# Differential attention scores: distance and mask added by VectorE in the pass that takes the row maximum, the first map scaled by ScalarE

## The chip, the cores and the metric

One core of a Trainium2 chip runs the whole program. The metric is device time in microseconds (us); lower is better. TensorE multiplies, VectorE and ScalarE do the elementwise work, GpSimd and SyncE here mostly issue transfers. PSUM has 8 banks of 128 x 512 float32, which only TensorE's results need; everything else lies in SBUF.

## What is computed

Two transformer blocks on x (512 tokens x 1024). The change is in the differential attention of the second block, 8 heads, each with two maps of 64 dimensions:

```python
dist = (tpos[:, None] - kpos[None, :]).astype(jnp.float32)
bias = -slopes[:, None, None] * dist               # slopes: 2 ** -(head + 1)
s = jnp.einsum("bhmqd,bhmkd->bhmqk", qblk, kt).astype(jnp.float32) * scale
s = s + bias[None, :, None]
s = jnp.where(dist >= 0, s, -jnp.inf)
p = jax.nn.softmax(s, axis=-1)
a = (p[:, :, 0] - lam * p[:, :, 1]).astype(vt.dtype)
return jnp.einsum("bhqk,bhkd->bhqd", a, vt)
```

Around it the second block has a convolution of 31 taps over 1024 channels, a cross-attention to a memory of 256 tokens, and projections.

## The kernel before

All work is laid out by hand: each engine has its own list of instructions, in order, and semaphores between them. A weight chunk (128 columns of a 1024-row matrix) is loaded into one of four raw buffers by SyncE, split by ScalarE into a hi part (`wh`, L1102) and by VectorE into a lo part (`wl`, L1760), and multiplied by TensorE in three matmuls for each of its 8 pieces (L463 to L465). Four chunks have split buffers, so the split of a chunk follows the use of the one four places ahead of it.

The differential stage runs over 8 heads j (0 to 7), and in each over 4 tiles tt of 128 queries; a unit is u = 4j + tt and has w = 128 (tt + 1) keys and two maps m. TensorE's list (L828 to L849) puts the pieces of five weight chunks between the attention steps of a head: the queries and keys of the next head, the gate of the previous one, and two for the convolution's input. Ahead of tiles 0 and 2 stand the scores of two tiles at once (`diff_scores`, L788): three float32 matmuls for each map (L800), then one for each map that adds slope times distance from two rows in float16 (L804), then one that adds the causal mask in the last 128 columns (L807), which closes the bank. In tiles 1 and 2 it sums squares of the next head's queries and keys (L529, waiting for `squared`), in tile 1 it multiplies the previous head by its values; it transposes each unit's probabilities (L677, waiting for `prob_ready`) a tile later. A bank 2 to 5 holds one map of one unit.

VectorE's list for a unit (L2203 to L2264): negated maximum of each map (L2214); in tile 3 the lo parts of the next head's keys and queries (L2125, L2131); in tile 0 the lo part of an older output (L1891); in tiles 0 to 2 four steps of the convolution (`conv`, L2173, 512 columns each); then it waits until both exponentials have emptied their banks, takes the reciprocals of both sums in one instruction (L2235), multiplies the second by minus lambda (L2236), scales the first map (L2238) and adds the second (L2239). After that come the lo part of the previous unit's transposed probabilities (L1942), weight chunks (L1760), in tile 2 the lo part of the values (L1887, waiting for ScalarE's hi part L1329) and the next head's normalised queries and keys (L2137). `then` makes VectorE wait for its own instruction.

ScalarE's list (L1518 to L1574): both exponentials with their sums (L1546), then the copy of the previous unit's transposed probabilities (L1324); after these in tiles 0 and 1 the copy of new queries or keys (L1250) and their squares (L1485), in tile 2 the roots (L1128, L1130, each with a table load) and the hi part of the values (L1329), in tile 3 ahead of the exponentials the hi parts of keys and queries (L1480, L1481); weight chunks (L1102) in all tiles.

Of the kernel before, what the change touches and what calls it, by code (L numbers as in the profile page):

```python
# [26 lines left out]
F32R = mybir.dt.float32r  # L27
F16 = mybir.dt.float16
BF16 = mybir.dt.bfloat16
# [5 lines left out]
P = 128  # L35
# [16 lines left out]
K_IDENT, K_ONES, K_FREQ, K_BLOCKS, K_SEL = 0, 128, 256, 257, 385  # L52
K_COLS = 385 + 4 * P

# [83 lines left out]
for _h in range(4):  # L138
# [6 lines left out]
    "const_in": "identity, ones and frequencies loaded", "rows_in": "packed vectors loaded",  # L145
    "tables_in": "masks, distances, slopes and blocks loaded",
    "mem_in": "memory loaded", "x_in": "x loaded", "bcast_in": "lambdas and sinks loaded on every partition", "late_in": "positions, gate bias and gain",
# [14 lines left out]
    "v_hi": "values: hi", "v_lo": "lo", "memk_hi": "memory's keys of a head: hi", "memk_lo": "lo",  # L162
    "negmax": "negated row maxima", "expd": "exponentials of sinks", "prob_ready": "units' probabilities",
    "pt_hi": "units' transposed probabilities: hi", "tanhed": "tanh of gates' arguments", "mixed": "gated outputs in mx",
# [49 lines left out]
def constants():  # L214
    k = np.zeros((P, K_COLS), np.float32)
    b = np.zeros((P, 3 * P), np.float32)
    h = np.zeros((P, S + 8 * P), np.float32)
    i = np.arange(P)
    k[:, K_IDENT:K_IDENT + P] = np.eye(P)
    k[:, K_BLOCKS:K_BLOCKS + P] = (i[:, None] // HD) == (i[None, :] // HD)  # L220
    k[:, K_ONES:K_ONES + P] = 1.0
    b[:, 0:P] = np.where(i[None, :] > i[:, None], 0.0, MASKED)
    b[:, P:2 * P] = np.where(i[None, :] <= i[:, None], 0.0, MASKED)
    b[:, 2 * P:3 * P] = np.eye(P)
    for n in range(8):
        for part in range(2):
            k[HD * (n % 2) + 32 * part + n, K_SEL + n // 2 * P:K_SEL + n // 2 * P + P] = 1.0
    j = np.arange(S)
    for half in (0, HD):
        h[half, 0:S], h[half + 1, 0:S] = j - (S - P), -1.0  # L230
        for n in range(8):
            cols = slice(S + n * P, S + n * P + P)
            h[half, cols], h[half + 1, cols] = 2.0 ** -(n + 1), i * 2.0 ** -(n + 1)
    k[:, K_FREQ] = (10000.0 ** (-(i % (HD // 2)).astype(np.float64) / (HD // 2))).astype(np.float32)
    return k, b.astype(mybir.dt.np(BF16)), h.astype(mybir.dt.np(F16))

# [87 lines left out]
def build(nc, t, out):  # L324
    ctx = ExitStack()
    with ctx:
# [15 lines left out]
        def sem(name):  # L342
# [30 lines left out]
        ident_b = sb("ident_b", [P, P], BF16)  # L373
        dist, slopes, blocks, xk = shared([("dist", [P, S], F16), ("slopes", [P, 8, P], F16), ("blocks", [P, P], F32)],
                                          [("xk", [P, 2, 2, MEM], F32R)])
        vt = sb("vt", [P, VT_COLS])
# [77 lines left out]
        def _(pe):  # L454
# [151 lines left out]
            def unit_scores(u_):  # L606

                if u_ >= FOX:
                    if u_ % 2 == 0:
                        banded_scores(u_)  # L610
                    return
                c, r = divmod(u_, 8)
                if r in (1, 2, 3, 5, 7):
                    return
                if r == 0:
                    pe.wait_ge(s.q_lo, c + 1)
                    banks.wait_empty(pe, ("ka", c))
                if u_ == 0:
                    pe.wait_ge(s.cum_done, 1)
                    pe.wait_ge(s.sel_in, 16)  # L620
                    pe.wait_ge(s.tables_in, 16 * 5)
                tiles = (0, 1) if r == 0 else (r // 2,)
                for side in range(2):
                    banks.open(pe, 2 + side, ("S", u_ + side))
                for n, tt in enumerate(tiles):
                    at, w = scores_at(u_ + 2 * n)
                    q_ = slice(tt * P, tt * P + P)
                    for q, k in ((0, 1), (1, 0), (0, 0)):
                        for side in range(2):
                            half = slice(HD * side, HD * side + HD)  # L630
                            pe.matmul(ps[2 + side][:, at:at + w], qd[c % 2][half, q, q_], kp[c % 2][half, k, 0:w],  # L631
                                      start=(n, q, k) == (0, 0, 1), stop=n > 0, **({"skip_group_check": True} if n else {}))
                    for side in range(2):
                        half = slice(HD * side, HD * side + HD)
                        pe.matmul(ps[2 + side][:, at:at + w], sel[half, c, :], negcum[half, 0:w], start=False, stop=True,
                                  **({"skip_group_check": True} if n else {}))
                for n, tt in enumerate(tiles):
                    at, w = scores_at(u_ + 2 * n)
                    for side in range(2):
                        ins = pe.matmul(ps[2 + side][:, at + w - P:at + w], ident_b[:], masks[:, 1, :], start=False, stop=True,  # L640
                                        skip_group_check=True)
                        if n == len(tiles) - 1:
                            banks.close(ins, ("S", u_ + side))
                        else:
                            banks.where["S", u_ + 2 + side] = banks.where["S", u_ + side]
# [142 lines left out]
            def diff_scores(j, first):  # L788
# [5 lines left out]
                for u_, w, q_ in units:  # L794
                    for m in range(2):
                        banks.open(pe, 2 + 2 * (u_ % 2) + m, ("D", u_, m))
                    for n, (q, k) in enumerate(((0, 1), (1, 0), (0, 0))):
                        for m in range(2):
                            half = slice(HD * m, HD * m + HD)
                            pe.matmul(outs[u_, m], qd[j % 2][half, q, q_], kd[half, j % 2, k, 0:w], start=n == 0, stop=False)  # L800
                for u_, w, q_ in units:
                    for m in range(2):
                        half = slice(HD * m, HD * m + HD)
                        pe.matmul(outs[u_, m], slopes[half, j, :], dist[half, S - w:S], start=False, stop=True)  # L804
                for u_, w, q_ in units:
                    for m in range(2):
                        ins = pe.matmul(outs[u_, m][:, w - P:w], ident_b[:], masks[:, 1, :], start=False, stop=True,  # L807
                                        skip_group_check=True)
                        banks.close(ins, ("D", u_, m))

# [188 lines left out]
        def _(pool):  # L999
# [10 lines left out]
            pool.dma_start(ident_b[:], t["consts_b"][:, 2 * P:3 * P]).then_inc(s.tables_in, 16)  # L1010
            pool.dma_start(dist[:], t["consts_h"][:, 0:S]).then_inc(s.tables_in, 16)
            pool.dma_start(slopes[:].rearrange("p a n -> p (a n)"), t["consts_h"][:, S:S + 8 * P]).then_inc(s.tables_in, 16)
            pool.dma_start(blocks[:], t["consts"][:, K_BLOCKS:K_BLOCKS + P]).then_inc(s.tables_in, 16)
# [71 lines left out]
        def _(act):  # L1085
# [432 lines left out]
            for j in range(8):  # L1518
                for tt in range(4):
# [16 lines left out]
                    for m in range(2):  # L1536
# [7 lines left out]
                        else:  # L1544
                            banks.wait_full(act, pt_key(UNITS - 1))
                        banks.empty(act.activation(prob[:, u_ % 2 if m == 0 else 2, 0:w], ps[banks.where[key][0]][:, 0:w],  # L1546
                                                   ACT.Exp, bias=stat[:, 0, col:col + 1],
                                                   accum_out=stat[:, 1, col:col + 1]), key)
                    if u_ > 0:
                        diff_pt_hi(u_ - 1)  # L1550
# [165 lines left out]
        def _(dve):  # L1716
# [484 lines left out]


            for j in range(8):  # L2203
                for tt in range(4):
# [6 lines left out]
                    for m in range(2):  # L2211
                        col = (2 * u_ + m) % 16
                        banks.wait_full(dve, ("D", u_, m))
                        dve.reduce_max(stat[:, 0, col:col + 1], bank(("D", u_, m))[:, 0:w], AX, negate=True)\  # L2214
                           .then_inc(s.negmax, 1)
                    if j and tt == (2 if j < 7 else 1):
# [9 lines left out]
                    if tt < 3:  # L2226
                        conv(4, j if tt else j - 1)
                    if (j, tt) == (7, 0):
                        diff_pt_lo(u_ - 1)

                    col = 2 * u_ % 16
                    r = stat[:, 2, col:col + 2]
                    for m in range(2):
                        banks.wait_empty(dve, ("D", u_, m))
                    then(dve.reciprocal(r, stat[:, 1, col:col + 2]))  # L2235
                    then(dve.tensor_tensor(r[:, 1:2], r[:, 1:2], nlam, ALU.mult))  # L2236
                    p0 = prob[:, u_ % 2, 0:w]
                    then(dve.tensor_scalar(p0, p0, r[:, 0:1], None, ALU.mult))  # L2238
                    dve.scalar_tensor_tensor(p0, prob[:, 2, 0:w], r[:, 1:2], p0, ALU.mult, ALU.add)\  # L2239
# [270 lines left out]
```

## Time and profile before

| | us |
|---|---|
| median of 3 runs | 1177.5 (1177.03 to 1178.06) |
| the profiled execution | 1176.51 |
| its span, first to last instruction | 1174.7 |
| TensorE busy in the span | 1141.0 |
| VectorE busy | 815.1 |
| ScalarE busy | 586.9 |

The granted clock of TensorE is 0.996 on average. The differential stage lies between 417 and 705 us of the span; its heads 2 to 6 each take some 36.7 us. In a profile's row the first number is the start, the second the time until the end of the last instruction that is merged into it; an idle time of the engine before the row stands in brackets with what ended it. Matmuls overlap, so what one costs is read from the start of the next.

### The profile page before, as it was taken

The numbers are of one execution on the slowest core, as the hardware profiler recorded it, in microseconds if no ns is written. First come the engines' busy times: TensorE is split into PE (matmuls) and PEld (weight loads), VectorE is DVE, ScalarE is ACT, GpSimd is POOL, SyncE is SP. The second block draws the span as 40 slices with busy tenths as digits, with TensorE's granted clock in tenths as the row PEclk, the third lists the DMA queues.
The fourth block names the chain that finished last, engine by engine and source line by source line (L and its number), as shares of the span: only waits on it lengthen the run. The fifth ranks groups of instructions, "written<-read, shape, count | busy, mean of one in ns | idle before, by whom it ended". The sixth has DMA issues, their size and how long they took to land.

```text
span 1174.7 us, 16788 instructions
## 1 busy us (share of the span) xinstructions
PE 1141.0 (97%) x6375; PEld 948.0 (81%) x6380; DVE 815.1 (69%) x1352; ACT 586.9 (50%) x1064; POOL 64.2 (5%) x73
## 2 busy tenths in 40 slices
PE   5899999999999999999999999999999999999998
PEld 5899777766899977777777778888888888788898
DVE  5788555668575237888898885898788686853351
ACT  5663455456564455766657655324554223651320
POOL 1029400101000000000000000000000000000000
PEclk9899999999999999999999999999999999999999
DMA  9967222321454322212222143232222323223221
GB/s 343 345 223 273 91 72 73 90 63 37 148 180 157 108 72 72 72 37 90 72 90 73 36 144 126 72 108 90 90 73 84 132 81 109 97 73 108 104 85 46
DMA packets 36208, 130.41 MB, mean 111 GB/s; under 512 B 4272, under 2 KB 6576, under 8 KB 35616
## 3 DMA queue, kind: packets, MB, share of 16 engines
q1 hardware_dynamic: 32560, 112.74, 29.0%
q0 software_dynamic: 3280, 16.29, 4.2%
q8 instruction: 51, 0.84, 0.3%
q10 hardware_dynamic: 288, 0.31, 0.1%
q14 instruction: 29, 0.24, 0.1%
HBM read 121.72 MB, written 6.29 MB: 109 GB/s over the span
## 4 chain that ended last, share of the span: by engine, by line
PE 87%; DVE 6%; ACT 3%; issue 2%; DMA 2%; SPq 0%; POOL 0%; DVEq 0%; ACTq 0%
PE bank L463 26%; PE bank L465 25%; PE bank L464 25%; PE bank L529 2%; PE bank L677 2%; DMA raw<-in_chunks 2%; DVE wl L1760 1%; PE bank L800 1%; PE bank L705 1%; PE bank L631 1%; ACT qf L1164 1%; DVE ca L2173 1%; DVE stat L1915 0%; PE bank L807 0%; DVE cumt L2441 0%
## 5 line engine op out<-in xcount | busy, mean ns | idle before, releaser
L463 PE MATMUL bank<-hl,wh 128*128 128x512 f32 x888 | 361.7, 407 | 0.9 <-DVE u L2187 0.9
L465 PE MATMUL bank<-hh,wh 128*128 128x512 f32 x888 | 347.1, 391 | 0.0
L464 PE MATMUL bank<-hh,wl 128*128 128x512 f32 x888 | 346.2, 390 | 0.0
L1102 ACT ACTIVATE wh<-raw 128x1024 fp32r<-128x1024 f32 x185 | 191.1, 1057 | 188.9 <-PE bank L465 178.1
L1760 DVE TENSOR_TENSOR wl<-raw,wh 128x1024 fp32r<-128x1024 f32 x185 | 225.2, 1242 | 84.5 <-ACT wh L1102 84.1
L463 PEld LDWEIGHTS bank<-hl,wh 128*128 128x128 f32 x888 | 167.2, 188 | 37.9 <-issue 4.8
L465 PEld LDWEIGHTS bank<-hh,wh 128*128 128x128 f32 x888 | 166.6, 188 | 36.4
L464 PEld LDWEIGHTS bank<-hh,wl 128*128 128x128 f32 x888 | 167.3, 188 | 33.6 <-issue 3.1
L2173 DVE SCALAR_TENSOR_TENSOR ca<-u,vt,ca 128x512 f32<-128x512 f32 x232 | 157.9, 745 | 0.0
L464 PE MATMUL bank<-oh,wl 128*128 128x512 f32 (+1 forms) x256 | 93.9, 367 | 0.0
L465 PE MATMUL bank<-oh,wh 128*128 128x512 f32 (+1 forms) x256 | 93.9, 367 | 0.0
L463 PE MATMUL bank<-wl,hh 128*128 128x256 f32 x320 | 91.6, 286 | 0.7 <-DVE hl L2089 0.7
L464 PE MATMUL bank<-wh,hl 128*128 128x256 f32 x320 | 90.5, 283 | 0.0
L465 PE MATMUL bank<-wh,hh 128*128 128x256 f32 x320 | 90.5, 283 | 0.0
L463 PE MATMUL bank<-ol,wh 128*128 128x512 f32 x192 | 75.5, 393 | 0.0
L463 PEld LDWEIGHTS bank<-wl,hh 128*128 128x128 f32 x320 | 61.4, 192 | 1.8 <-issue 1.8
L464 PEld LDWEIGHTS bank<-wh,hl 128*128 128x128 f32 x320 | 61.4, 192 | 0.5 <-issue 0.5
L465 PEld LDWEIGHTS bank<-wh,hh 128*128 128x128 f32 x320 | 61.4, 192 | 0.0
L1546 ACT ACTIVATE prob<-bank,stat 128x128 f32<-128x128 f32 (+3 forms) x64 | 33.1, 523 | 49.2 <-DVE stat L2214 48.5
L463 PE MATMUL bank<-wl,oh 128*128 128x256 f32 x192 | 55.7, 290 | 1.0 <-DVE ytok L2050 0.7
L464 PEld LDWEIGHTS bank<-oh,wl 128*128 128x128 f32 x256 | 49.7, 194 | 8.0 <-issue 0.5
L465 PEld LDWEIGHTS bank<-oh,wh 128*128 128x128 f32 x256 | 49.5, 193 | 7.5
(323 smaller groups left out, 1676.2 us busy)
## 6 DMA issues: line engine op xcount, KB each, us to landing
raw<-in_chunks SPq DMA_DIRECT2D x193, 512.0 KB, 3.7
ada_a<-in_chunks SPq DMA_DIRECT2D x8, 512.0 KB, 10.9
ada_b<-in_chunks SPq DMA_DIRECT2D x8, 512.0 KB, 8.6
x<-in_x POOLq DMA_DIRECT2D x4, 512.0 KB, 10.5
mem_scratch<-kvm POOLq DMA_DIRECT2D x1, 2048.0 KB, 8.2
x<-in_x POOLq DMA_DIRECT2D x1, 2048.0 KB, 8.1
x_scratch<-x POOLq DMA_DIRECT2D x1, 2048.0 KB, 7.7
kvm<-mem_scratch POOLq DMA_DIRECT2D x1, 2048.0 KB, 9.5
```

What stands on the lines that cost most here:

```text
L463: pe.matmul(o, a[0], b[1], start=start, stop=False, **kw)
L464: pe.matmul(o, a[1], b[0], start=False, stop=False, **kw)
L465: return pe.matmul(o, a[0], b[0], start=False, stop=stop, **kw)
L529: ins = pe.matmul(ps[bank][:, 0:n], ones_[:], x_, start=i == 0, stop=i == len(squares) - 1)
L631: pe.matmul(ps[2 + side][:, at:at + w], qd[c % 2][half, q, q_], kp[c % 2][half, k, 0:w], start=(n, q, k) == (0, 0, 1), stop=n > 0, **({"sk ...
L677: ins = pe.transpose(ps[b][:, n * P:n * P + P], blk, ident[:])
L705: ins = pe.matmul(ps[7][half, cols], v_, p_, start=kb == 0, stop=True, skip_group_check=True)
L800: pe.matmul(outs[u_, m], qd[j % 2][half, q, q_], kd[half, j % 2, k, 0:w], start=n == 0, stop=False)
L1102: act.activation(wh[:, SLOT[nxt]], raw[:, RAW_SLOT[nxt]], ACT.Copy).then_inc(s.w_hi, 1)
L1546: banks.empty(act.activation(prob[:, u_ % 2 if m == 0 else 2, 0:w], ps[banks.where[key][0]][:, 0:w], ACT.Exp, bias=stat[:, 0, col:col + 1] ...
L1760: dve.tensor_tensor(wl[:, w], raw[:, RAW_SLOT[nxt]], wh[:, w].bitcast(F32), ALU.subtract)\
L2173: ins = dve.scalar_tensor_tensor(dst, src, w, dst, ALU.mult, ALU.add)
```

## The change

The distances are no longer two float16 rows with a table of slopes, but one float32 table of 128 x 512: minus half the distance for head 0, and -1e30 where a key is behind its query. VectorE adds it to the scores: one instruction (`tensor_tensor_reduce`) writes minus the sum back to PSUM and takes the minimum of it, which is the negated maximum. The exponential takes the scores with scale -1. After tile 3's pass of each head but the last, VectorE halves the table. TensorE's matmuls with slopes and mask go, and each score bank closes with the last of its own three matmuls. On VectorE the four convolution steps of tiles 0 to 2 become 1, 1 and 2, with the first reciprocal between the first two and the second behind the second; ScalarE, behind both exponentials, waits for the first reciprocal and scales the first map; VectorE waits for that ahead of the combination. One of the five transfers of tables is gone. In the diff the lines on imports and the names of signals are left out:

```diff
-    j = np.arange(S)
-    for half in (0, HD):
-        h[half, 0:S], h[half + 1, 0:S] = j - (S - P), -1.0
-        for n in range(8):
-            cols = slice(S + n * P, S + n * P + P)
-            h[half, cols], h[half + 1, cols] = 2.0 ** -(n + 1), i * 2.0 ** -(n + 1)
+    back = i[:, None] + (S - P) - np.arange(S)[None, :]
+    k[:, K_DIST:K_DIST + S] = np.where(back >= 0, -0.5 * back, MASKED)
...
                     for n, (q, k) in enumerate(((0, 1), (1, 0), (0, 0))):
                         for m in range(2):
                             half = slice(HD * m, HD * m + HD)
-                            pe.matmul(outs[u_, m], qd[j % 2][half, q, q_], kd[half, j % 2, k, 0:w], start=n == 0, stop=False)
-                for u_, w, q_ in units:
-                    for m in range(2):
-                        half = slice(HD * m, HD * m + HD)
-                        pe.matmul(outs[u_, m], slopes[half, j, :], dist[half, S - w:S], start=False, stop=True)
-                for u_, w, q_ in units:
-                    for m in range(2):
-                        ins = pe.matmul(outs[u_, m][:, w - P:w], ident_b[:], masks[:, 1, :], start=False, stop=True,
-                                        skip_group_check=True)
-                        banks.close(ins, ("D", u_, m))
+                            ins = pe.matmul(outs[u_, m], qd[j % 2][half, q, q_], kd[half, j % 2, k, 0:w],
+                                            start=n == 0, stop=n == 2)
+                            if n == 2:
+                                banks.close(ins, ("D", u_, m))
...
-            pool.dma_start(dist[:], t["consts_h"][:, 0:S]).then_inc(s.tables_in, 16)
-            pool.dma_start(slopes[:].rearrange("p a n -> p (a n)"), t["consts_h"][:, S:S + 8 * P]).then_inc(s.tables_in, 16)
+            pool.dma_start(dist[:], t["consts"][:, K_DIST:K_DIST + S]).then_inc(s.tables_in, 16)
...
                         banks.empty(act.activation(prob[:, u_ % 2 if m == 0 else 2, 0:w], ps[banks.where[key][0]][:, 0:w],
-                                                   ACT.Exp, bias=stat[:, 0, col:col + 1],
+                                                   ACT.Exp, scale=-1.0, bias=stat[:, 0, col:col + 1],
                                                    accum_out=stat[:, 1, col:col + 1]), key)
+                    p0 = prob[:, u_ % 2, 0:w]
+                    act.wait_ge(s.first_r, u_ + 1)
+                    act.activation(p0, p0, ACT.Copy, scale=stat[:, 2, 2 * u_ % 16:2 * u_ % 16 + 1]).then_inc(s.scaled, 1)
                     if u_ > 0:
                         diff_pt_hi(u_ - 1)
...
+            dve.wait_ge(s.tables_in, 16 * 4)
...
                         banks.wait_full(dve, ("D", u_, m))
-                        dve.reduce_max(stat[:, 0, col:col + 1], bank(("D", u_, m))[:, 0:w], AX, negate=True)\
-                           .then_inc(s.negmax, 1)
+                        scores = bank(("D", u_, m))[:, 0:w]
+                        dve.tensor_tensor_reduce(scores, scores, dist[:, S - w:S], -1.0, -MASKED, ALU.add, ALU.min,
+                                                 stat[:, 0, col:col + 1]).then_inc(s.negmax, 1)
+                    if tt == 3 and j < 7:
+                        then(dve.tensor_scalar(dist[:], dist[:], 0.5, None, ALU.mult))
...
                     if tt < 3:
-                        conv(4, j if tt else j - 1)
+                        conv(1, j if tt else j - 1)
+
+                    col = 2 * u_ % 16
+                    r = stat[:, 2, col:col + 2]
+                    banks.wait_empty(dve, ("D", u_, 0))
+                    dve.reciprocal(r[:, 0:1], stat[:, 1, col:col + 1]).then_inc(s.first_r, 1)
+                    if tt < 3:
+                        conv(1, j if tt else j - 1)
+                    banks.wait_empty(dve, ("D", u_, 1))
+                    then(dve.reciprocal(r[:, 1:2], stat[:, 1, col + 1:col + 2]))
+                    then(dve.tensor_tensor(r[:, 1:2], r[:, 1:2], nlam, ALU.mult))
+                    if tt < 3:
+                        conv(2, j if tt else j - 1)
                     if (j, tt) == (7, 0):
                         diff_pt_lo(u_ - 1)
-
-                    col = 2 * u_ % 16
-                    r = stat[:, 2, col:col + 2]
-                    for m in range(2):
-                        banks.wait_empty(dve, ("D", u_, m))
-                    then(dve.reciprocal(r, stat[:, 1, col:col + 2]))
-                    then(dve.tensor_tensor(r[:, 1:2], r[:, 1:2], nlam, ALU.mult))
                     p0 = prob[:, u_ % 2, 0:w]
-                    then(dve.tensor_scalar(p0, p0, r[:, 0:1], None, ALU.mult))
+                    dve.wait_ge(s.scaled, u_ + 1)
                     dve.scalar_tensor_tensor(p0, prob[:, 2, 0:w], r[:, 1:2], p0, ALU.mult, ALU.add)\
                        .then_inc(s.prob_ready, 1)
```

## Rows read from the trace of the kernel before

**Rows 1.** The page, chain that ended last: shares of the span by engine

```profile
PE 87%; DVE 6%; ACT 3%; issue 2%; DMA 2%; SPq 0%; POOL 0%; DVEq 0%; ACTq 0%
```

**Rows 2.** Busy time by stretches: from:to, us, busy of PE, PEld, DVE, ACT, POOL

```profile
417.00:656.00 239.00, 239.00 (x1233) 185.28 (x1233) 197.16 (x371) 154.40 (x286) 0.00 (x0) 1.00 0.23 73
656.00:705.00 49.00, 45.26 (x234) 35.49 (x233) 40.62 (x76) 28.07 (x52) 0.53 (x1) 1.00 0.28 97
```

**Rows 3.** TensorE in order of time, heads 5 and 6, last row head 7

```profile
593.53 0.34 PE L804 MATMUL bank<-dist,slopes 64*128 64x128 f16 x4
...
594.01 0.48 PE L463 MATMUL bank<-hl,wh 128*128 128x512 f32 x1
...
613.51 0.56 PE L804 MATMUL bank<-dist,slopes 64*128 64x384 f16 x4
...
614.23 1.08 PE L529 MATMUL bank<-norms,blocks 128*128 128x512 f32 x2
...
675.11 0.33 PE L677 MATMUL bank<-cst,prob 128*128 128x128 f32 x1 [2.17 <-DVE prob L2239]
```

**Rows 4.** VectorE in order of time: tiles 2 and 3, then tile 0

```profile
577.55 1.02 DVE L2214 TENSOR_REDUCE stat<-bank 128x1 f32<-128x384 f32 x2 [1.08 <-PE bank L807]
...
579.09 2.73 DVE L2173 SCALAR_TENSOR_TENSOR ca<-u,vt,ca 128x512 f32<-128x512 f32 x4
...
586.47 0.69 DVE L1887 TENSOR_TENSOR vv<-dv,vv 128x512 fp32r<-128x512 f32 x1 [2.93 <-ACT vv L1329]
...
591.94 0.16 DVE L2235 RECIPROCAL stat<-stat 128x2 f32<-128x2 f32 x1
...
592.33 0.49 DVE L2238 TENSOR_SCALAR prob<-prob,stat 128x512 f32<-128x512 f32 x1
592.85 0.75 DVE L2239 SCALAR_TENSOR_TENSOR prob<-prob,stat 128x512 f32<-128x512 f32 x1
...
596.97 1.41 DVE L2173 SCALAR_TENSOR_TENSOR ca<-u,vt,ca 128x512 f32<-128x512 f32 x2
```

**Rows 5.** Waits from 400 to 720 us: who <- whom: total, times, longest

```profile
DVE stat L2214 <- PE bank L807: 8.5, 7, 1.8
```

**Rows 6.** TensorE's weight loads in order of time, heads 3 and 5

```profile
529.40 0.19 PEld L463 LDWEIGHTS bank<-hl,wh 128*128 128x128 f32 x1 [0.30 <-DVE wl L1760]
...
601.19 0.42 PEld L529 LDWEIGHTS bank<-norms,blocks 128*128 128x128 f32 x2
```

**Rows 7.** TensorE from 612.7 to 612.8 us: the last score matmuls of tile 2

```profile
612.46 0.51 PE L800 MATMUL bank<-kd,qk 64*128 64x384 f32 x4
```

**Rows 8.** VectorE: a tensor_tensor_reduce and its read in time; a scan's group

```profile
57.34 0.22 DVE L1802 CUSTOM_DVE_ANT_0 gj<-lam 128x64 f32<-128x64 f32 x1
57.49 0.08 DVE L1802 DVE_READ_ACCUMULATOR2_ANT sc<- 128x1 f32 x1
...
L1849 DVE TENSOR_TENSOR_SCAN cumt<-cumt 128x512 f32<-128x512 f32 x1 | 1.2, 1225 | 0.0
```

**Rows 9.** Single lines: duration ns min/median/max, first and last start, forms

```profile
L2214 DVE TENSOR_REDUCE stat<-bank x64: 279/482/686, 418.3 to 696.2; 128x1 f32<-128x128 f32 x16, 128x1 f32<-128x256 f32 x16, 128x1 f32<-128x384 f32 x16, 128x1 f32<-128x512 f32 x16
...
L2238 DVE TENSOR_SCALAR prob<-prob,stat x32: 286/387/489, 420.0 to 698.3; 128x128 f32<-128x128 f32 x8, 128x256 f32<-128x256 f32 x8, 128x384 f32<-128x384 f32 x8, 128x512 f32<-128x512 f32 x8
...
L1546 ACT ACTIVATE prob<-bank,stat x64: 357/523/690, 418.7 to 697.0; 128x128 f32<-128x128 f32 x16, 128x256 f32<-128x256 f32 x16, 128x384 f32<-128x384 f32 x16, 128x512 f32<-128x512 f32 x16
```

**Rows 10.** ScalarE in order of time: tiles 2 and 3, then tile 0

```profile
579.27 0.38 ACT L1324 ACTIVATE pth<-bank 128x256 fp32r<-128x256 f32 x1
...
588.52 0.63 ACT L1480 ACTIVATE kd<-qf 128x512 fp32r<-128x512 f32 x1 [0.66 <-DVE qf L2137]
589.06 0.61 ACT L1481 ACTIVATE qk<-qf 128x512 fp32r<-128x512 f32 x1
...
596.99 0.60 ACT L1324 ACTIVATE pth<-bank 128x512 fp32r<-128x512 f32 x1
...
599.84 0.64 ACT L1485 ACTIVATE norms<-qf 128x512 f32<-128x512 f32 x1
```

More of the change, by code:

```diff
@@ L27 @@
 F32R = mybir.dt.float32r
-F16 = mybir.dt.float16
 BF16 = mybir.dt.bfloat16
@@ L52 @@
 K_IDENT, K_ONES, K_FREQ, K_BLOCKS, K_SEL = 0, 128, 256, 257, 385
-K_COLS = 385 + 4 * P
+K_DIST = 385 + 4 * P
+K_COLS = K_DIST + S
 VEC_ROWS = [("c", 8), ("b_ada", 16), ("g_pre", 8), ("norm_g", 8), ("mem_g", 8), ("dw_b", 8), ("ln_g", 8),
@@ L145 @@
     "const_in": "identity, ones and frequencies loaded", "rows_in": "packed vectors loaded",
-    "tables_in": "masks, distances, slopes and blocks loaded",
+    "tables_in": "masks, distances and blocks loaded",
     "mem_in": "memory loaded", "x_in": "x loaded", "bcast_in": "lambdas and sinks loaded on every partition", "late_in": "positions, gate bias and gain",
@@ L162 @@
     "v_hi": "values: hi", "v_lo": "lo", "memk_hi": "memory's keys of a head: hi", "memk_lo": "lo",
-    "negmax": "negated row maxima", "expd": "exponentials of sinks", "prob_ready": "units' probabilities",
+    "negmax": "negated row maxima", "first_r": "units' first reciprocal sums", "scaled": "units' first maps over their sums", "expd": "exponentials of sinks", "prob_ready": "units' probabilities",
     "pt_hi": "units' transposed probabilities: hi", "tanhed": "tanh of gates' arguments", "mixed": "gated outputs in mx",
@@ L216, in constants @@
     b = np.zeros((P, 3 * P), np.float32)
-    h = np.zeros((P, S + 8 * P), np.float32)
     i = np.arange(P)
@@ L227, in constants @@
             k[HD * (n % 2) + 32 * part + n, K_SEL + n // 2 * P:K_SEL + n // 2 * P + P] = 1.0
-    j = np.arange(S)
-    for half in (0, HD):
-        h[half, 0:S], h[half + 1, 0:S] = j - (S - P), -1.0
-        for n in range(8):
-            cols = slice(S + n * P, S + n * P + P)
-            h[half, cols], h[half + 1, cols] = 2.0 ** -(n + 1), i * 2.0 ** -(n + 1)
+    back = i[:, None] + (S - P) - np.arange(S)[None, :]
+    k[:, K_DIST:K_DIST + S] = np.where(back >= 0, -0.5 * back, MASKED)
     k[:, K_FREQ] = (10000.0 ** (-(i % (HD // 2)).astype(np.float64) / (HD // 2))).astype(np.float32)
-    return k, b.astype(mybir.dt.np(BF16)), h.astype(mybir.dt.np(F16))
+    return k, b.astype(mybir.dt.np(BF16))
 def packed_vectors(inputs):
@@ L373, in build @@
         ident_b = sb("ident_b", [P, P], BF16)
-        dist, slopes, blocks, xk = shared([("dist", [P, S], F16), ("slopes", [P, 8, P], F16), ("blocks", [P, P], F32)],
-                                          [("xk", [P, 2, 2, MEM], F32R)])
+        dist, blocks, xk = shared([("dist", [P, S], F32), ("blocks", [P, P], F32)], [("xk", [P, 2, 2, MEM], F32R)])
         vt = sb("vt", [P, VT_COLS])
@@ L620, in unit_scores @@
                     pe.wait_ge(s.sel_in, 16)
-                    pe.wait_ge(s.tables_in, 16 * 5)
+                    pe.wait_ge(s.tables_in, 16 * 4)
                 tiles = (0, 1) if r == 0 else (r // 2,)
@@ L2499 @@
         given(name, np.ascontiguousarray(inputs[name]))
-    consts, consts_b, consts_h = constants()
+    consts, consts_b = constants()
     given("consts", consts)
     given("consts_b", consts_b)
-    given("consts_h", consts_h)
     given("vectors", packed_vectors(inputs))
```

## The prediction

> **What bounds the kernel now.** I read the chain of waits first: TensorE carries 87% of it and VectorE 6% [rows 1]. Then the table by stretches [rows 2]: in the differential stage the first stretch (heads 0 to 6) has TensorE busy 239.00 of 239.00 us, the second (the last head) only 45.26 of 49.00. So TensorE is the bound for seven heads, and in the last one something else ends last; the row that shows it is TensorE idle for 2.17 us until VectorE's combined probabilities [rows 3]. "Busy" doesn't say how near the other engines are, so the third view is VectorE's line in order of time: per head it waits about 1.1 us for the scores of tile 2, and in the same tile 2.93 us for ScalarE's values [rows 4]; the table of waits sums the first to 8.5 us in 7 waits [rows 5]. The last is TensorE's weight loads: in head 3 one waited 0.30 us for VectorE's lo chunk [rows 6], so that VectorE and ScalarE run a loop about as long as TensorE's head (some 36.7 us, from the tile-2 maximum at 577.55 to the scores at 614.2). That near tie decides this change.
>
> **TensorE: what it sheds.** Per head two groups of matmuls with the slopes and the mask go: 594.01 - 593.53 = 0.48 us and 614.23 - 613.51 = 0.72 us, together 1.20 us [rows 3]; over 8 heads 9.6 us. The maximum of tile 2 comes sooner still: its bank now closes on its own score matmuls, which end at 612.46 + 0.51 = 612.97 [rows 7], not behind tile 3's and both masks at 614.2. Tile 2's maximum so gains 1.25 us against TensorE's start of the pair.
>
> **VectorE: what it takes on.** The maximum becomes one pass that adds, negates and reduces, and writes the scores back to PSUM. The nearest row is the same instruction over 64 columns: 0.22 us, its accumulator read starts 0.15 us behind it and is 0.08 us long, so that it ends 0.01 us behind the pass [rows 8]. A plain maximum lasts 0.28 us for 128 columns and 0.69 for 512 [rows 9], so 64 columns would last about 0.21: the same time per column in both, and the read beside its tail. Lower bound 0 (it streams the same columns), upper the scan, 1.23 us for 512 columns [rows 8]; nothing in the trace writes PSUM from VectorE. I take 0.01 us each, nearest to the same instruction. Added too: a second reciprocal (0.16 us long, about 0.09 of issue), and the halving of the distances, 0.52 us with its wait (as the scaling of 512 columns, 592.33 to 592.85), once per head. Gone is the first map's scaling, 0.29 to 0.49 us [rows 9]. In sum VectorE's work hardly changes. The order does.
>
> **The new wait.** ScalarE now stops in its own order after the second exponential until VectorE's first reciprocal, and VectorE does that behind one convolution step. Queued behind it on ScalarE are the copy of the previous unit's transposed probabilities, the next squares, roots, split values and weight chunks; VectorE and TensorE wait for those.
> Step one, tile 2 (head 4's times). The convolution starts at 579.09 and issues in (2.73 - 0.75) / 3 = 0.66 (four in 2.73, one of 512 columns lasting 0.75); reciprocal 0.16, signal 0.04: ScalarE goes on at 579.95 rather than 579.27, a wait of 0.68 [rows 4, 10]. Its scaling of 384 columns takes about 0.43 (copies of 512 follow each other by 589.06 - 588.52 = 0.54, less 0.11 per 128 columns as the exponentials differ) [rows 9, 10]. The values, for which VectorE waits anyway, come 1.11 us later.
> Step two, tile 3. The halving puts 0.52 ahead of the split of keys and queries. From the reciprocal to the combination it was 592.85 - 591.94 = 0.91; through ScalarE it is 0.16 + 0.04 + 0.62 + 0.03 = 0.85. Net +0.46.
> Step three, tile 0 of the next head. Reciprocal behind split and convolution: 596.97 + 0.66 + 0.16 + 0.04 = 597.83 rather than 596.99 [rows 4, 10], so 0.84 of wait, and 0.22 for 128 columns. ScalarE's square of the new queries, which ended at 599.84 + 0.64 = 600.48 [rows 10], is late by 1.11 + 0.46 + 1.06 = 2.63 us against the tile-2 maximum.
> TensorE sums that square: its weight load for it starts at 601.19 [rows 6], so 0.7 us are spare. The rest stalls TensorE. From tile-2 maximum to tile-2 maximum the loop changes by 2.63 - 0.7 - 1.25 = +0.7 us per head. VectorE's own loop (1.11 + 0.46 less 0.2 in tile 0 and 0.15 in tile 1, so +1.2 against its 1.1 of waiting) and TensorE's 35.5 us are both shorter. So TensorE's saving is paid into the longer loop.
>
> **The sum.** Heads 0 and 1 are not in the loop: no convolution stands there before the reciprocal until head 1's tile 1. Tile 2's maximum of head 1 comes earlier by 0.48 + 0.72 + 0.48 + 1.25, less 0.1 for head 0's halving: -2.8 us. Five loops to head 6: +3.5; the 0.3 us for which head 3 already waits is not paid twice: so +0.4. From head 6's tile 2 on VectorE is the bound, as before: 1.11 + 0.46 - 0.2 - 0.3 = +1.0. In the last tiles ScalarE's late weight chunk costs 0.5 (0.08 + 0.43) and the last combination, no longer behind VectorE's scaling, returns 0.5. End of the stage: +1.4; some 38 passes on the path with 0.01: +0.4. After it TensorE is the bound again and carries +1.8 to the end. The profiled execution took 1176.51 us, 1.8 beyond its span, and the median lies 1.0 above it; I add to the median: 1177.5 + 1.8 = 1179.3 us. The 9.6 us of matmul are hidden by nothing; they are lost to waits.
>
> The tables are one transfer fewer on GpSimd's queue, and the removed transfers were all landed long before the stage: nothing.
>
> **A rule that speaks against it.** Where VectorE streams two float32 operands, the trace shows no loss: the combination of the two maps reads two from SBUF and passes 512 columns in 0.75 us [rows 4], hardly longer than a maximum of 512, with one operand (0.69) [rows 9]. The Trainium skill (Vector Engine (DVE) Microarchitecture Reference, "Points that are easy to get wrong") says that the scalar-tensor-tensor family with two SBUF sources that aren't bf16 runs at half the throughput, as no port is left for the accumulator. The combination's row speaks against it without an accumulator, and the 64-column row with one [rows 8]; the new pass has one source in PSUM. By the rule the time would be that of the first rival.
>
> **Rivals.**
> *The new pass is slow* (slower). If it runs as the scan does, each pass costs 0.13, 0.27, 0.41 or 0.54 more. In the loop lie two each of tiles 2, 3 and 0: 2 x (0.41 + 0.54 + 0.13) = 2.2 us per head, 11 over five, and some 4 in the last one and a half: 1179 + 15 = 1194. Milder, if the accumulator read's 0.08 is not hidden: 38 x 0.08 = +3: 1182. It decides from 0.02 us per pass, where the sum leaves "no change". For it: no row writes PSUM. Against: the 64-column row.
> *The matmuls are saved* (faster). If the waits of ScalarE have more cover than I read, TensorE stays the bound up to head 6: 7 x 1.20 + 0.5 = 8.9 less 1.0: about 1169.6. For it: 239.00 of 239.00 busy. Against: the load that already waits in head 3.
> *The reciprocal doesn't hold ScalarE* (faster). Were steps one and three without their waits (0.68 and 0.84), the loop would change by 2.63 - 1.52 - 1.95 = -0.8; then the next loops bind, VectorE's own at -0.5: 1179.3 - 5 x 1.2 - 0.7, about 1173.
>
> **How the numbers follow.** Forecast, near 1179: 0.47 (of it 0.38 within 0.2%, 0.09 above). Slow pass: 0.20 mild, 0.08 at half rate. All matmuls saved: 0.12. No hold: 0.13. Faster by over 0.2% (2.4 us, about what a measurement of this kernel can tell from no change): 0.12 + 0.13 = 0.25; within: 0.38; slower: 0.09 + 0.28 = 0.37. The range leaves out the half rate (0.08) and all matmuls saved (0.12): 1173 to 1186, the upper end for a pass dearer by 0.2 us. Cases of both signs are in it; the forecast's own range is 1177 to 1182.
>
> **What would show it.** Right: no slopes or mask matmuls in the stage; ScalarE idle before its scaling until VectorE's reciprocal, about 0.7 us in tile 2 and 0.8 in tile 0; TensorE, without idle time before, idle for 1 to 2 us ahead of its sums of squares in heads 2 to 6; VectorE no longer waiting for tile 2's scores more than 0.5 us; the new pass 0.28 to 0.69 us long. Wrong: a pass over 0.8 us for 512 columns, a head of TensorE near 35.5 us, or ScalarE's scaling starting at once.

## The result and the profile after

The changed kernel takes 1181.59 us (median of 5 runs, 1180.52 to 1183.18) against 1177.03 for the kernel before, run beside it (5 runs, 1176.00 to 1178.06): a ratio of 1.0042, 95% interval 1.0027 to 1.0056. It is slower by 0.4%. The profiled execution took 1180.52 with a span of 1178.7, 4.0 longer than before's 1174.7.

First the chain that ended last, by engine, from the page of the kernel after; then its table by stretches (from:to, us, busy of PE, PEld, DVE, ACT, POOL, granted clock, DMA share, GB/s):

```profile
PE 73%; DVE 13%; ACT 7%; issue 5%; DMA 2%; SPq 0%; POOL 0%; ACTq 0%; DVEq 0%
```

```profile
417.00:656.00 239.00, 232.13 (x1107) 177.72 (x1108) 191.61 (x426) 165.35 (x309) 0.00 (x0) 1.00 0.22 73
656.00:705.00 49.00, 43.43 (x210) 33.72 (x209) 38.94 (x87) 32.31 (x59) 0.54 (x1) 1.00 0.27 97
```

TensorE's share of the chain falls from 87% to 73% [rows 1], and where it was busy for all of 239.00 us [rows 2] it now has 6.87 us idle. VectorE is busy 5.55 us less there, ScalarE 10.95 more. So TensorE got its matmuls off and then waits for the other two. ScalarE's line in order of time (after; head 4's tiles 2 and 3 and head 5's tile 0; the bracket is the idle time before the row and what ended it) shows where:

```profile
579.52 0.20 ACT L1533 ACTIVATION_READ_ACCUMULATOR prob<-bank,stat 128x1 f32 x1
580.27 0.62 ACT L1538 ACTIVATE prob<-prob,stat 128x384 f32<-128x384 f32 x1 [0.56 <-DVE stat L2226]
580.80 0.36 ACT L1311 ACTIVATE pth<-bank 128x256 fp32r<-128x256 f32 x1
...
594.17 0.72 ACT L1538 ACTIVATE prob<-prob,stat 128x512 f32<-128x512 f32 x1 [0.89 <-DVE stat L2226]
594.80 0.47 ACT L1311 ACTIVATE pth<-bank 128x384 fp32r<-128x384 f32 x1
...
599.11 0.20 ACT L1533 ACTIVATION_READ_ACCUMULATOR prob<-bank,stat 128x1 f32 x1
600.03 0.40 ACT L1538 ACTIVATE prob<-prob,stat 128x128 f32<-128x128 f32 x1 [0.72 <-DVE stat L2226]
600.34 0.58 ACT L1311 ACTIVATE pth<-bank 128x512 fp32r<-128x512 f32 x1
```

Before, the copy of transposed probabilities followed the second exponential at once [rows 10]. Now L1538 stands between them, waits for VectorE's reciprocal (L2226), and holds ScalarE 0.53, 0.63 and 0.31 us for its own work. VectorE's line (after, the same heads) has both new instructions in it:

```profile
577.82 0.57 DVE L2206 CUSTOM_DVE_ANT_0 bank<-bank,dist 128x384 f32<-128x384 f32 x1 [0.38 <-PE bank L794]
578.30 0.14 DVE L2206 DVE_READ_ACCUMULATOR2_ANT stat<- 128x1 f32 x1
578.30 0.60 DVE L2206 CUSTOM_DVE_ANT_0 bank<-bank,dist 128x384 f32<-128x384 f32 x1
...
587.98 0.69 DVE L1877 TENSOR_TENSOR vv<-dv,vv 128x512 fp32r<-128x512 f32 x1 [4.51 <-ACT vv L1316]
...
592.30 0.42 DVE L2209 TENSOR_SCALAR dist<-dist 128x512 f32<-128x512 f32 x1
592.76 0.69 DVE L2115 TENSOR_TENSOR kd<-qf,kd 128x512 fp32r<-128x512 f32 x1
...
593.98 0.16 DVE L2226 RECIPROCAL stat<-stat 128x1 f32<-128x1 f32 x1
...
594.99 0.75 DVE L2238 SCALAR_TENSOR_TENSOR prob<-prob,stat 128x512 f32<-128x512 f32 x1 [0.60 <-ACT prob L1538]
```

The wait for the scores falls from 1.08 to 0.38 us, the wait for ScalarE's values rises from 2.93 to 4.51 [rows 4]. And TensorE, without idle time there before [rows 3], waits in three places of each head (after, head 5):

```profile
594.11 0.95 PE L794 MATMUL bank<-kd,qk 64*128 64x128 f32 x12 [0.36 <-DVE qk L2121]
598.34 0.47 PE L457 MATMUL bank<-hl,wh 128*128 128x512 f32 x1 [0.55 <-DVE u L2177]
603.87 1.13 PE L523 MATMUL bank<-norms,blocks 128*128 128x512 f32 x2 [0.48 <-ACT norms L1472]
```

From one start of tile 2's scores to the next a head lasts 36.69 to 36.71 us before (37.01 once) and 37.71 to 37.76 after (37.89 once).

### The profile page after: what moved, and what is told of

Its sections match the earlier page's. It is cut to its first block, busy times and chain, and to the rows that moved or that the text cites. A ratio compares the mean times of both kernels' runs of the same rounds, so it can differ in the third digit from the quotient of the medians.

```text
span 1178.7 us, 16642 instructions
## 1 busy us (share of the span) xinstructions
PE 1136.3 (96%) x6247; PEld 942.0 (80%) x6252; DVE 809.6 (69%) x1423; ACT 604.6 (51%) x1096; POOL 63.0 (5%) x72
## 4 chain that ended last, share of the span: by engine, by line
PE 73%; DVE 13%; ACT 7%; issue 5%; DMA 2%; SPq 0%; POOL 0%; ACTq 0%; DVEq 0%
PE bank L457 22%; PE bank L459 22%; PE bank L458 22%; DVE wl L1750 2%; PE bank L523 2%; DMA raw<-in_chunks 2%; PE bank L671 2%; ACT wh L1089 1%; DVE ca L2163 1%; DVE bank L2206 1%; PE bank L699 1%; ACT norms L1115 1%; PE bank L625 1%; ACT L1115 1%; DVE qf L2127 1%
## 5 line engine op out<-in xcount | busy, mean ns | idle before, releaser
L2163 DVE SCALAR_TENSOR_TENSOR ca<-u,vt,ca 128x512 f32<-128x512 f32 x232 | 160.5, 746 | 0.6
L459 PE MATMUL bank<-wh,oh 128*128 128x256 f32 x192 | 54.9, 286 | 0.0
```

The costliest lines, as they stand in the source:

```text
L459: return pe.matmul(o, a[0], b[0], start=False, stop=stop, **kw)
L2163: ins = dve.scalar_tensor_tensor(dst, src, w, dst, ALU.mult, ALU.add)
```

## The experiments

Each kernel was run 5 or 11 times beside the kernel before. Profiled executions differ by up to 2.3 us in when the stage begins (its first scores start at 416.59 us in e2 and 418.85 in e8), so heads are compared by their length on TensorE: the mean of four, from the start of head 2's tile-2 scores to that of head 6's. The time is the median; the ratio is to before, with its 95% interval.

| kernel | us | ratio | head |
|---|---|---|---|
| before | 1176.8 to 1177.5 | 1 | 36.78 |
| after | 1181.59 | 1.0042 (1.0027 to 1.0056) | 37.77 |
| e1: reciprocal ahead of the convolution | 1176.05 | 0.9993 (0.9984 to 1.0003) | 36.86 |
| e2: scaling back on VectorE | 1173.06 | 0.9966 (0.9953 to 0.9978) | 36.43 |
| e3: before, scaling on ScalarE | 1187.09 | 1.0086 (1.0072 to 1.0099) | 38.33 |
| e4: before without the matmuls | 1169.91 | 0.9936 (0.9924 to 0.9949) | 35.81 |
| e5: scaling of 32 columns | 1176.14 | 0.9992 (0.9983 to 1.0000) | 36.95 |
| e6: no halving | 1178.38 | 1.0014 (1.0005 to 1.0022) | 37.29 |
| e7: no halving, plain maximum | 1177.10 | 0.9998 (0.9990 to 1.0007) | 37.09 |
| e8: e2, tile 1's steps moved | 1173.19 | 0.9964 (0.9951 to 0.9978) | 36.27 |
| e9: e2, tile 0's steps moved | 1170.78 | 0.9942 (0.9930 to 0.9955) | 35.90 |
| e10: before, tile 0's steps moved | 1175.63 | 0.9985 (0.9976 to 0.9994) | 36.69 |

### e1: the hold alone

```diff
-                    if tt < 3:
-                        conv(1, j if tt else j - 1)
                     banks.wait_empty(dve, ("D", u_, 0))
                     dve.reciprocal(r[:, 0:1], stat[:, 1, col:col + 1]).then_inc(s.first_r, 1)
                     if tt < 3:
-                        conv(1, j if tt else j - 1)
+                        conv(2, j if tt else j - 1)
```

> The changed kernel with the first reciprocal ahead of the first convolution step (in place of one step before it, two stand behind it). Theory A, the loop through ScalarE is what eats the matmuls' saving: in head 4 of the changed kernel ScalarE waits 0.66 us in tile 2 and 0.84 in tile 0 for this reciprocal, both mostly vanish, the loop falls by about 1.2 us per head; over six loops that is up to 7, less what the next bound takes (TensorE, whose saving is 1.2 per head): about 1175, with TensorE's wait for the squares gone. Rival B, VectorE's own additions (two longer passes, halving) set the loop: the order of reciprocal and convolution changes nothing there, within 1 us of 1181.6. Rival C: VectorE now idles until the exponential is done and loses what ScalarE wins: 1180 to 1182 with new idle time of 0.3 us or more ahead of the reciprocal.

Theory A: 0.91 us per head and 5.5 us in all went with one instruction's place. ScalarE's line (e1, head 4's tiles 2 and 3, head 5's tile 0) shows no idle time before the scaling in tiles 2 and 0 any more; in tile 3, where no convolution stands ahead of the reciprocal, it stays:

```profile
577.43 0.62 ACT L1538 ACTIVATE prob<-prob,stat 128x384 f32<-128x384 f32 x1
...
591.31 0.72 ACT L1538 ACTIVATE prob<-prob,stat 128x512 f32<-128x512 f32 x1 [0.88 <-DVE stat L2223]
...
596.51 0.40 ACT L1538 ACTIVATE prob<-prob,stat 128x128 f32<-128x128 f32 x1
```

TensorE's wait for the squares is gone, as expected. It still waits 0.34 us in head 5 for the convolution's input (L2177), which VectorE empties behind tile 3's combination; that one waits 0.61 for ScalarE's scaling. In heads 3 and 5 it also waits 0.41 and 0.20 us for ScalarE's copy of the previous head's output (L1496).

### e2: the whole of ScalarE's part undone

```diff
-                    p0 = prob[:, u_ % 2, 0:w]
-                    act.wait_ge(s.first_r, u_ + 1)
-                    act.activation(p0, p0, ACT.Copy, scale=stat[:, 2, ...]).then_inc(s.scaled, 1)
...
+                    then(dve.reciprocal(r, stat[:, 1, col:col + 2]))
+                    then(dve.tensor_tensor(r[:, 1:2], r[:, 1:2], nlam, ALU.mult))
+                    then(dve.tensor_scalar(p0, p0, r[:, 0:1], None, ALU.mult))
```

> The changed kernel with the scaling of the first map back on VectorE: four convolution steps in a row, both reciprocals in one instruction, minus lambda, scaling, combination, as in the kernel before; the new pass, the halving and the removed matmuls stay. Theory A (ScalarE's wait and scaling, 0.66 + 0.53 us in tile 2 and 0.84 + 0.31 in tile 0, make the loop longer than TensorE's head): both go, TensorE is the bound again up to head 6 at some 35.5 us per head, and about 1.2 us in each of seven heads come back, less what VectorE loses in the last head: about 1171. Rival B, VectorE's passes and halving are the cost: VectorE has now more work than in either kernel (per head 0.3 to 0.5 us of scaling in each of four tiles beside 0.42 of halving), and the time is 1180 or above.

Faster than both kernels, by 0.34% against before: the direction is theory A's. The size isn't: heads last 36.0 to 36.85 us, not 35.5, and 2 us are missing. e4, e8 and e9 say why.

### e3: ScalarE's part alone

```diff
+                    p0 = prob[:, u_ % 2, 0:w]
+                    act.wait_ge(s.first_r, u_ + 1)
+                    act.activation(p0, p0, ACT.Copy, scale=stat[:, 2, ...]).then_inc(s.scaled, 1)
```

(with the reciprocals between the convolution steps, as in the change)

> The kernel before with the scaling of the first map on ScalarE and the reciprocals between the convolution steps, exactly as in the changed kernel; matmuls with slopes and mask, and the plain maximum, stay. Theory A: the squares come late by 1.2 (tile 2) + 1.15 (tile 0) = 2.35 us, 0.7 of it is spare, so 1.65 us per head over five or six loops, 8 to 10 less 0.3: about 1186. Rival B (ScalarE's part is covered, the pass and the halving cost): within 2 us of 1177.

Theory A, at 1187.09 for "about 1186". Heads last 38.3 us, 1.63 above the 36.70 of before's undisturbed heads, and TensorE waits for the squares (0.45) and for VectorE's split of queries (0.38), though it has all its matmuls still. The scaling on ScalarE by itself costs about 10 us.

### e4: the matmuls alone

```diff
-                        pe.matmul(outs[u_, m], slopes[half, j, :], dist[half, S - w:S], start=False, stop=True)
...
-                        ins = pe.matmul(outs[u_, m][:, w - P:w], ident_b[:], masks[:, 1, :], start=False, stop=True,
-                                        skip_group_check=True)
```

> The kernel before without the matmuls that add slopes times distances and the causal mask, so that its scores have neither; nothing else differs. It shows what TensorE's saving is worth where no other engine takes anything on. If TensorE is the bound through seven heads: 7 x 1.20 + 0.5 = 8.9 us, about 1168. If the loop of ScalarE and VectorE is about as long as TensorE's head already (head 3's load waits 0.30 us), the loop too becomes shorter by 1.25 through the earlier maximum of tile 2, so the same 1168; if the loop binds elsewhere, 1171 or above.

The saving is worth 6.9 us, not 8.9, and a head on TensorE is 35.75, not 35.5: 0.95 saved, not 1.20. TensorE's line shows the pairs of tile 0 and tile 2, first before, then in e4 with what follows:

```profile
592.73 0.96 PE L800 MATMUL bank<-kd,qk 64*128 64x128 f32 x12
...
612.18 1.49 PE L800 MATMUL bank<-kd,qk 64*128 64x384 f32 x12
```

```profile
588.72 0.96 PE L800 MATMUL bank<-kd,qk 64*128 64x128 f32 x12
589.61 0.50 PE L463 MATMUL bank<-hl,wh 128*128 128x512 f32 x1
...
607.74 1.49 PE L800 MATMUL bank<-kd,qk 64*128 64x384 f32 x12
609.16 1.12 PE L529 MATMUL bank<-norms,blocks 128*128 128x512 f32 x2
```

From the scores to the next matmul it is 0.89 and 1.42 us in e4; before, the slopes' matmuls started after 0.80 and 1.33 (593.53 and 613.51 in [rows 3]): what now follows the scores starts 0.09 later than the removed group did, so the two removals are worth 0.39 and 0.63. The sums of squares behind take 0.05 more (0.96 to the next row, 0.91 before).

### e5: the scaling's length

```diff
-                    p0 = prob[:, u_ % 2, 0:w]
+                    p0 = prob[:, u_ % 2, 0:P // 4]
```

> The changed kernel with ScalarE scaling only the first 32 columns of each first map (the rest stays unscaled); the wait for the reciprocal and all else stay. It takes the scaling's length apart from its wait. The rows give 0.40, 0.62 and 0.72 us for 128, 384 and 512 columns, so some 0.33 for 32: 0.3 less in tile 2, 0.4 in tile 3 (through the combination and what VectorE does behind it), 0.07 in tile 0. Theory A1 (waits and scaling both lie in the loop): 0.35 to 0.75 us less per head, over five or six heads 2 to 4: 1177.5 to 1179.5. Rival: only the wait for the reciprocal holds the loop, the scaling itself is covered: 1181 to 1182.

More than theory A1 asked: 0.82 us per head. ScalarE's wait in tile 2 is the same, the scaling 0.32 long for 32 columns (e5):

```profile
579.43 0.32 ACT L1538 ACTIVATE prob<-prob,stat 128x32 f32<-128x32 f32 x1 [0.56 <-DVE stat L2226]
579.66 0.36 ACT L1311 ACTIVATE pth<-bank 128x256 fp32r<-128x256 f32 x1
```

Of after's lengths 0.30 (tile 2), 0.40 (tile 3) and 0.08 (tile 0) go, together 0.78. The head became shorter by as much as the three lengths together, so the scaling lies in the loop with its full length in all three tiles.

### e6 and e7: the halving and the pass

The first line is e6; e7 also goes back to the plain maximum:

```diff
-                        then(dve.tensor_scalar(dist[:], dist[:], 0.5, None, ALU.mult))
...
-                        dve.tensor_tensor_reduce(scores, scores, dist[:, S - w:S], -1.0, -MASKED, ALU.add, ALU.min,
-                                                 stat[:, 0, col:col + 1]).then_inc(s.negmax, 1)
+                        dve.reduce_max(stat[:, 0, col:col + 1], scores, AX, negate=True).then_inc(s.negmax, 1)
```

> The changed kernel without the halving of the distances, so that all heads take the first head's slope. In the trace it holds VectorE 0.46 us in tile 3, ahead of the split of keys and queries for which TensorE waits 0.36 us there. Theory A (it lies in the loop with its full length): 0.46 less per head, five or six heads, 2.3 to 2.8: about 1179. Rival (the later waits of 0.55 for the convolution's input and 0.48 for the squares take it up): 1181 to 1182.

> As the run without the halving, and the pass that adds, negates and reduces is the plain maximum of before (so no distance and no mask is added at all, and the exponential takes the scores as they are). Two passes of a unit then issue some 0.06 us sooner, three units of a loop 0.18: about 1.0 us below the run without the halving, about 1178. If the new pass were the main cost of the change (the first rival of the prediction), this run would come to 1172 or lower; if the accumulator's reading and the writing to PSUM were covered, it would be equal to the run without the halving.

Without the halving a head is 0.48 us shorter: it lies in the loop with its full length. Without the new pass it is 0.20 shorter again and the time lower by 1.28 us, or 0.03 for each of some 38 passes (the prediction's count): not hidden, and not the main cost either.

### e8 and e9: what bounds the version without ScalarE's part

Both start from e2 and move four convolution steps into VectorE's wait for ScalarE's values in tile 2: e8 those that end tile 1, e9 those of tile 0. First the line that e8 changes, then e9's; the two lines added to tile 2 are the same in both:

```diff
-                    if tt == 1:
+                    if tt == 1 and j == 7:
                         conv(4, j)
...
-                    if tt < 3:
+                    if tt in (1, 2) or (j, tt) == (7, 0):
                         conv(4, j if tt else j - 1)
...
                     if tt == 2:
+                        if j < 7:
+                            conv(4, j)
                         split_v(1 + j, dv[:, :, j * P:j * P + P])
```

> The version with the scaling back on VectorE, where in heads 0 to 6 the four convolution steps that end tile 1 stand instead in tile 2, right ahead of the split of the values, where VectorE waits 2.93 us for ScalarE's values in that version (four steps issue in 2.66). Theory: in that version VectorE's loop (from the maximum of tile 2 through ScalarE's values back to it, 36.4 us, no other wait in it) ends last by a little, and TensorE's head would be some 35.5; moved into the wait the steps cost nothing, VectorE again waits for tile 2's scores by 1 us or more, and six heads become 0.9 us shorter: 1167 to 1168. Rival: TensorE, busy for 238.67 of 239.00 us in the heads 0 to 6 of that version, is the bound there already: no change, 1173.

No change against e2: my theory of e2 fell. VectorE (e8, head 4's tile 2) now waits long for TensorE, so the loop back to its own maximum wasn't what ended last:

```profile
575.13 0.57 DVE L2203 CUSTOM_DVE_ANT_0 bank<-bank,dist 128x384 f32<-128x384 f32 x1 [2.15 <-PE bank L794]
```

Nor is it the rival, since TensorE's weight loads (e8, head 5's tile 0) still wait for VectorE:

```profile
601.26 0.19 PEld L457 LDWEIGHTS bank<-hl,wh 128*128 128x128 f32 x1 [0.44 <-DVE wl L1747]
```

That lo chunk stands behind everything VectorE does from ScalarE's values on, and tile 1's steps come after it. Such waits stand only ahead of tile 2 of heads 3 and 5, and the stretches that hold them last 36.68 and 36.39 us; those of 36.02 have none. So:

> The version with the scaling back on VectorE, where in heads 0 to 6 the four convolution steps of tile 0 (instead of those that end tile 1) stand in tile 2 ahead of the split of the values. In the run with tile 1's steps moved VectorE waited 2.15 us for tile 2's scores, so its loop was shorter than TensorE's head, and yet TensorE's heads lasted 36.0 to 36.7 us, not the 35.75 that they last where only the matmuls are gone: a weight load waited 0.44 us for VectorE's lo chunk in tile 0, which stands behind that tile's four steps. Theory: from ScalarE's values to that lo chunk VectorE works without a wait, and this stretch sets TensorE's head; without the four steps in it (2.7 us) the lo chunk is in time, heads last 35.75, six heads become 0.3 to 0.6 us shorter than in the version with the scaling back alone: 1170 to 1171. Rival: what lengthens TensorE's heads is not this chunk: 1173.

As expected: 1170.78 us, 0.58% below before, and the fastest of those that leave nothing out. TensorE is busy throughout heads 0 to 6 again (e9):

```profile
417.00:656.00 239.00, 239.00 (x1149) 185.84 (x1149) 209.06 (x441) 161.56 (x293) 0.00 (x0) 1.00 0.22 73
```

Its heads last 35.87 to 35.96 us, 0.12 above e4's 35.75, which was not taken apart. The move brings every product of that stretch sooner (in e8 TensorE's weight loads waited for probabilities too, 0.87 us in head 3), so it shows that tile 0's four steps cost the time there, not that the lo chunk alone did.

### e10: the same move before

The edit is e9's, in the kernel before.

> The same move of tile 0's four convolution steps in the kernel before, nothing else. There TensorE has no idle time in heads 0 to 6, with heads of 36.70 us, and one of 37.01: only that one can become shorter, by 0.3: 1176.5 to 1177, no difference that shows. If VectorE's order had any part in the other heads of before, 1175 or lower.

1175.63, 1.9 us below the median beside it (0.7 to 2.8 by the interval), where at most 1.0 was expected. In the traces the head of 37.01 fell to 36.66 and the last one from 35.11 to 34.72, 0.74 together; the others stayed at 36.69 or 36.70. The rest of the 1.9 isn't located, and 0.4 of the difference of the two profiled executions lies ahead of the stage. So the move explains 0.7 to 1.9 us of e9's gain, and the rest of e9's edits (matmuls removed, new pass, halving) some 4.9 (1175.63 - 1170.78).

## Why the prediction was right or wrong

The forecast was 1179.3, the result 1181.59. The spans differ by 4.0 us and the medians by 4.6, where the sum said 1.8. The time lies in the range, which was wide enough for more than twice the sum; slower by over 0.2% had a chance of 0.37, against 0.38 for no such difference. The mechanism was the one forecast (e1 to e3 and e5), and its size per head was short.

*Up to head 1's tile 2*: -2.8 us forecast, -2.72 measured (467.15 to 464.43 us).

*The loop.* Forecast: 0.68 us per head and 0.06 for six passes, 0.74. Measured: 37.77 less the undisturbed 36.70, 1.07 (0.99 against before's mean of 36.78, in which the wait of 0.30 in head 3 counts; the sum takes that off by itself). The runs take it apart, in this order:

| term, us per head | forecast | run | |
|---|---|---|---|
| scaling on ScalarE with its waits | 1.11 - 0.06 + 1.06 - 0.7 = 1.41 | 1.63 | e3 less 36.70 |
| halving | 0.52 | 0.48 | after less e6 |
| six passes | 0.06 | 0.20 | e6 less e7 |
| matmuls gone, maximum of tile 2 earlier | -1.25 | -1.24 | e7 less e3 |
| sum | 0.74 | 1.07 | |

Two terms were mis-sized. The first is ScalarE's scaling. Its waits were right: from 0.09 behind the start of the accumulator's read, where the next row would start, to the scaling it is 0.66 us in tile 2 (0.68 forecast) and 0.83 in tile 0 (0.84). Its length was taken from copies of 512 columns, 0.62 long, as 0.43 for 384 and 0.22 for 128; it is 0.53 and 0.31. In tile 3 I set 0.85 from the reciprocal to the combination; it is 594.99 - 593.98 = 1.01, as the 512 columns take 0.72 and the combination starts 0.10 behind them, not 0.03. So the rows make the term 0.08 + 0.08 + 0.16 larger, the run 0.22. The difference of 0.10 fits the cover of 0.7 for the squares, which I counted up to a weight load at 601.19 [rows 6]: the matmul on the squares itself started at 601.42, so the cover may have been 0.8 (before):

```profile
601.42 1.02 PE L529 MATMUL bank<-norms,blocks 128*128 128x512 f32 x2
```

That is worked out by difference; no run tests it. The second term is the pass: 0.03 instead of 0.01 each. That is the size of the first rival's milder form, which I let count from 0.02 per pass: it is real and brings 1.28 us by e7. But its reason isn't borne out, since the accumulator's read lies beside the next pass, and that the result is near its 1182 is luck: it took 3 us for the passes.

With 0.33 more over five loops the shift at head 6's tile 2 is +2.30 instead of about +0.7 (the sum's +0.4 and 0.3 of passes). From there to the end of the stage +1.7, where 1.1 was said (1.0 and 0.1); the 0.6 more was not taken apart.

*The signs.* Right: ScalarE's waits, VectorE's wait for tile 2's scores at 0.38 us (no more than 0.5 said), and the pass 0.29 to 0.74 long (0.69 was the upper end). Wrong: that TensorE's idle time, 1.39 us in head 5, would all stand ahead of the squares. It is 0.48 there; 0.36 stands ahead of tile 0's scores and 0.55 ahead of a piece whose bank VectorE empties only behind tile 3's combination (L2177). I followed one product of the loop to TensorE, where three come late by turns; the shift per loop was added up without them.

*The rivals.* "All matmuls saved" was put at 1169.6 and is near the time when the other two engines take nothing on (e4, 1169.91) or when the scaling and tile 0's steps are moved out of the loop (e9, 1170.78). That the times agree so closely is partly luck, as its step "1.20 us per head" was too large by 0.25: I priced removed matmuls by the starts of the rows behind them and didn't ask when the next kind of row would start. "The reciprocal doesn't hold ScalarE" is e1: 1.2 us per head and about 1173 forecast, 0.91 and 1176.05 measured, as other waits remain. "Half rate": the row of the pass decides (after, 64 passes in four lengths: min, median and max in ns, first and last start, forms), at most 739 ns where the scan of 512 columns took 1.23 us [rows 8]:

```profile
L2206 DVE CUSTOM_DVE_ANT_0 bank<-bank,dist x64: 291/518/739, 418.2 to 700.5; 128x128 f32<-128x128 f32 x16, 128x256 f32<-128x256 f32 x16, 128x384 f32<-128x384 f32 x16, 128x512 f32<-128x512 f32 x16
```

The rule on two sources that aren't bf16 (the Trainium skill, Vector Engine (DVE) Microarchitecture Reference, "Points that are easy to get wrong") speaks of two sources in SBUF; here one lies in PSUM, and no halving shows.

## What to carry to other kernels

Where TensorE is 100% busy, ask how far the next loop is from it before counting a removed matmul as saved: here it was some 0.7 to 0.8 us per head, and a step that moved 0.29 to 0.49 us of work per unit to an engine that was busy for 154.40 of 239.00 us put its whole length into that loop in three tiles of each head, and its wait in two. An instruction handed to an engine with time to spare still stops that engine's list for its input, so place its producer as early as its own input allows (e1: 5.5 us for the place of one convolution step per unit), or leave it where it was (e2). And look where the loop has slack: the same convolution steps cost nothing in VectorE's wait for the values (e9), but only the steps that stand ahead of the late product are worth moving (e8).

## What the runs showed of the hardware

- ScalarE's scaling from SBUF to SBUF in place, with a factor per partition, lasts (after and e5) 0.32, 0.40, 0.51, 0.62 and 0.72 us for 32, 128, 256, 384 and 512 columns, where before's 512-column copies took 0.61 and 0.63 [rows 10].
- The pass that adds, negates and reduces, from PSUM and SBUF to PSUM, lasts 0.29, 0.43, 0.57 and 0.70 us for 128 to 512 columns (after), and 0.03 to 0.04 more where it follows another one whose accumulator is being read; that read is 0.14 us long (0.08 in the 64-column row of [rows 8]). Two passes of 384 columns issue in 1.00 us, two plain maxima in 0.94.
- A matmul group that is removed gives back less than the distance between the starts of the rows around it: 0.39 of 0.48 and 0.63 of 0.72 us, as the next group starts 0.09 later behind the float32 scores than the removed one did (e4 against before). Why it does is not shown.
